# Eight experts placed by token count, three of them in positions of 64 seats with two products per weight tile

## What is computed

```
logits = h @ w_router                      # 256 x 8
top_v, top_i = top_k(logits, 2)
combine = sum(one_hot(top_i) * softmax(top_v))
out = sum over e of combine[:, e] * ((silu(h @ w1[e]) * (h @ w3[e])) @ w2[e])
```

## Time and profile before

| | us |
|---|---|
| Median of 3 runs (1662.18 to 1662.34) | 1662.2 |
| Span of the profiled execution | 1660.5 |
| PE busy | 1644.2 |
| DVE busy | 1286.4 |
| ACT busy | 1058.6 |
| One pass of the experts' loop | 119.0 |

### The profile page before, as it was taken

How to read it: one execution, slowest core, us unless ns; L and a number is a source line. 1 busy time by engine, 2 the same in 40 slices (tenths; PEclk the granted TensorE clock), 3 DMA queues, 4 the chain that set the end, 5 groups by cost and what they waited for, 6 DMA issues and landing times.

```text
span 1660.5 us, 22803 instructions
## 1 busy us (share of the span) xinstructions
PE 1644.2 (99%) x8464; PEld 1397.3 (84%) x8464; DVE 1286.4 (77%) x1163; ACT 1058.6 (64%) x961; POOL 30.1 (2%) x57
## 2 busy tenths in 40 slices
PE   9999999999999999999999999999999999999997
PEld 8988889999899888788888888888888888888885
DVE  7575567555567747698888888988888888888997
ACT  6654445434465544577777777777777777777775
POOL 1000000000000000010000000000000000000100
PEclk9999999999999999999999999999999999999999
DMA  7753488885365444799999999999999999999994
GB/s 233 231 188 121 150 279 298 264 263 189 103 207 191 140 139 165 253 379 393 395 394 386 357 394 388 359 391 385 364 384 376 375 392 364 387 388 360 394 392 160
DMA packets 243426, 496.98 MB, mean 299 GB/s; under 512 B 8534, under 2 KB 64400, under 8 KB 243360
## 3 DMA queue, kind: packets, MB, share of 16 engines
q1 hardware_dynamic: 237360, 479.23, 80.3%
q0 software_dynamic: 2624, 8.45, 1.5%
q10 hardware_dynamic: 3376, 8.39, 1.3%
HBM read 476.64 MB, written 19.40 MB: 299 GB/s over the span
## 4 chain that ended last, share of the span: by engine, by line
PE 91%; DVE 3%; ACT 3%; issue 2%; DMA 1%; SPq 1%; DVEq 0%; POOL 0%; ACTq 0%
PE bank L1142 25%; PE bank L681 20%; PE bank L1175 19%; PE bank L1146 12%; PE bank L852 9%; PE bank L1159 1%; ACT whi L1423 1%; PE bank L671 1%; DVE wlo L1804 1%; PE bank L966 1%; DMA x_sb<-in_x 1%; DMA hn<-in_mem 1%; ACT pbuf L1558 0%; SPq L1297 0%; PE bank L938 0%
## 5 line engine op out<-in xcount | busy, mean ns | idle before, releaser
L2219 DVE TENSOR_TENSOR wlo<-raw,whi 128x2048 fp32r<-128x2048 f32 x328 | 748.2, 2289 | 108.1 <-ACT whi L1660 108.1
L1660 ACT ACTIVATE whi<-raw 128x2048 fp32r<-128x2048 f32 x328 | 627.8, 1918 | 177.5 <-PE bank L1146 93.7
L1804 DVE TENSOR_TENSOR wlo<-raw,whi 128x2048 fp32r<-128x2048 f32 (+3 forms) x121 | 259.3, 2148 | 175.8 <-ACT whi L1423 174.0
L1142 PE MATMUL bank<-whi,yT_hi 128*128 128x512 f32 x896 | 352.5, 396 | 0.0
L1142 PE MATMUL bank<-whi,yT_lo 128*128 128x512 f32 x896 | 347.4, 390 | 0.0
L1423 ACT ACTIVATE whi<-raw 128x2048 fp32r<-128x2048 f32 (+3 forms) x121 | 217.8, 1801 | 137.4 <-PE bank L681 100.5
L1146 PE MATMUL bank<-wlo,yT_hi 128*128 128x512 f32 x896 | 240.0, 390 | 0.0
L1146 PEld LDWEIGHTS bank<-wlo,yT_hi 128*128 128x128 f32 x896 | 168.2, 188 | 35.5
L1142 PEld LDWEIGHTS bank<-whi,yT_lo 128*128 128x128 f32 x896 | 168.3, 188 | 33.7 <-DVE yT_lo L2187 0.2
L1142 PEld LDWEIGHTS bank<-whi,yT_hi 128*128 128x128 f32 x896 | 168.3, 188 | 33.5
L1175 PE MATMUL bank<-whi,yT_hi 128*128 128x512 f32 x448 | 176.1, 393 | 0.0
(11 more groups left out here) (287 smaller groups left out, 2014.0 us busy)
## 6 DMA issues: line engine op xcount, KB each, us to landing
raw<-in_moe_w SPq DMA_DIRECT2D x336, 1024.0 KB, 7.4
raw<-in_w_in SPq DMA_DIRECT2D x36, 1024.0 KB, 5.2
raw<-in_dense_w SPq DMA_DIRECT2D x30, 1024.0 KB, 6.5
raw<-in_w_br SPq DMA_DIRECT2D x12, 1024.0 KB, 5.0
raw<-in_w_out SPq DMA_DIRECT2D x8, 1024.0 KB, 5.1
rows_by_slot<-qxT SPq DMA_DIRECT2D x15, 512.0 KB, 7.0
raw<-in_w_mkv SPq DMA_DIRECT2D x6, 1024.0 KB, 8.4
y_by_slot<-qxT SPq DMA_DIRECT2D x9, 512.0 KB, 7.7
```

The costliest lines, as they stand in the source:

```text
L1142: nc.tensor.matmul(b[:, :], hselT[a][:, half, tok(k)], w[:, k, :], start=(half + k + a == 0), stop=False)
L1660: nc.scalar.activation(whi[:, (E0 + n) % SPLIT, :], raw[:, n % RAW, :], ACT.Copy).then_inc(hi_ready, 1)
L1804: V.tensor_tensor(wlo[:, m % SPLIT, 0:size], raw[:, pieces[n][1], 0:size], whi[:, m % SPLIT, 0:size].bitcast(F32), ALU.subtract).then_inc( ...
L2219: V.tensor_tensor(wlo[:, s, :], raw[:, n % RAW, :], whi[:, s, :].bitcast(F32), ALU.subtract).then_inc(lo_ready, 1)
```

## The change

Experts are no longer taken in the order of their numbers. DVE counts each expert's tokens, ranks the experts (expert 0 is put first whatever its count) and gives the five highest the five positions marked H of `"HLHLHLHH"` and the three lowest the three marked L. SP reads the expert's number for each position from memory and loads that expert's weights.

An H position works as before. An L position has 64 seats: its stationary tile holds the high parts of 64 tokens in columns 0 to 63 and their low parts in columns 64 to 127. One matmul with `whi` and one with `wlo` then stand in for three, and the results of seat s and of seat s + 64 have to be added. For the hidden values that is done on PE: ACT and DVE copy both up products out of PSUM as they are, eight matmuls of 64 columns with the constant matrix `fold` transpose and add them, then ACT applies Silu (`silu_t`), DVE multiplies (`gated_t`), ACT makes the high part and DVE the low part. For the result y it is done by two matmuls with `fold` in the next position's first block. The loop is gone: all positions are written out. The part for tokens beyond an expert's seats (128 or 64) has 16 passes, and is run if any expert has such tokens.

The core of the diff:

```diff
+LIGHT = 64
+ROLES = "HLHLHLHH"
...
+                    if is_light(phase):
+                        order = [(k, 0) for k in range(4)]
...
+            def hidden_T(phase, b_, j=0):
+
+                read(pe, (phase, "e3", b_), j)
+                if is_light(phase):
+                    read(pe, (phase, "e1", b_))
+                    pe.wait_ge(fold_ready, 1)
+                b = claim((phase, "eT", b_), j)
+                if is_light(phase):
+                    for i, src in enumerate((silu_m, g32_m)):
+                        for c in range(BM):
+                            a = (i * BM + c) * LIGHT
+                            ins = nc.tensor.matmul(b[:, a:a + LIGHT], src[:, tok(c)], fold[:, 0:LIGHT],
+                                                   start=True, stop=True)
...
+                    terms = ((0, 0), (0, 1)) if is_light(phase) else ((0, 0), (1, 0), (0, 1))
...
+            def fold_result(p):
+
+                for n in range(2):
+                    read(pe, (p, "ey", n))
+                    b = claim((p, "yf", n))
+                    mark(nc.tensor.matmul(b[:, :], fold, y_slot[:, n * HALF:(n + 1) * HALF], start=True, stop=True),
+                         (p, "yf", n))
...
+            up(0, "w1", 0, 0, lambda half: read(pe, ("rows0", l, half)))
+            up(0, "w3", 0)
+            for p in range(NE):
+                blocks(p)
+                if p < LAST:
+                    up(p + 1, "w1", 0, 0, lambda half: read(pe, (p + 1, "rows", half)))
+                    hidden_T(p, NM - 1)
+                    up(p + 1, "w3", 0)
+                    down(p, NM - 1)
...
+            expert = {0: 0}
+            for n in range(HEAD + EARLY, N_E):
+                p = e_items[n][0]
+                if p not in expert:
+                    sp.wait_ge(order_known, 1)
+                    expert[p] = sp.value_load(order_i[0:1, p:p + 1], min_val=0, max_val=NE - 1)
+                load_item(n, expert[p])
...
             reached(pool, ("mT", 0, 3))
+            nc.gpsimd.memset(fold, 0.0).then_inc(pool_step, 1)
+            for i, shift in enumerate((0, LIGHT, -LIGHT)):
+                pool.wait_ge(pool_step, 3 + ROPE // 2 + i + 1)
+                ins = nc.gpsimd.affine_select(out=fold, in_=fold, compare_op=ALU.not_equal, fill=1.0, base=shift,
+                                              pattern=[[-1, P]], channel_multiplier=1)
+                ins.then_inc(pool_step, 1) if i < 2 else ins.then_inc(fold_ready, 1)
             for t in range(T):
...
+                free(nc.scalar.activation(silu_m, b[:, :], ACT.Copy if is_light(phase) else ACT.Silu), (phase, "e1", b_))
+
+            def silu_folded(p, b_):
+
+                b = full(act, (p, "eT", b_))
+                nc.scalar.activation(silu_t, b[:, 0:BM * LIGHT], ACT.Silu).then_inc(silu_t_ready, 1)
+
+            def hidden_hi(phase, b_, j=0):
+
+                if is_light(phase):
+                    read(act, (phase, "eT", b_))
+                    nc.scalar.activation(by_slot(gated_m[0][:, b_ % 2, :])[:, :, 0:LIGHT],
+                                         gated_t.rearrange("p (c s) -> p c s", c=BM), ACT.Copy).then_inc(g_hi, 1)
+                    return
...
+                    e_hi(e_room(phase, "e1", b_), j)
+                    if is_light(phase):
+                        e_hi(e_room(phase, "eT", b_ - 1), j)
+                        silu_folded(phase, b_ - 1)
...
+            b = full(dve, ("most", l))
+            free(V.tensor_copy(load, b[:, 0:NE]), ("most", l))
+            read(dve, ("most", l))
+            square_e = [P, NE, NE]
+            link(V.scalar_tensor_tensor(out=key_e, in0=iota_e[:, :], scalar=-1.0 / 16, in1=load, op0=ALU.mult, op1=ALU.add))
+            link(V.tensor_scalar(key_e[:, 0:1], key_e[:, 0:1], 4096.0, None, ALU.add))
+            link(V.tensor_tensor(pairs_e, key_e.unsqueeze(1).broadcast_to(square_e),
+                                 key_e.unsqueeze(2).broadcast_to(square_e), ALU.is_gt))
+            link(V.tensor_reduce(order_e, pairs_e, AX_X, ALU.add))
+            link(V.tensor_tensor(pairs_e, iota_e[:, :].unsqueeze(1).broadcast_to(square_e),
+                                 order_e.unsqueeze(2).broadcast_to(square_e), ALU.is_equal))
+            dve.wait_ge(seats, NE)
+            link(V.tensor_tensor(pairs_e, pairs_e, seat[:, :].unsqueeze(1).broadcast_to(square_e), ALU.mult))
+            link(V.tensor_reduce(pos_e, pairs_e, AX_X, ALU.add))
+            link(V.tensor_scalar(cap_e, order_e, float(HEAVY), float(LIGHT - CAP), ALU.is_ge, ALU.mult))
+            link(V.tensor_scalar(cap_e, cap_e, float(CAP), None, ALU.add))
+            link(V.tensor_tensor(hits_e, iota_e[:, :].unsqueeze(2).broadcast_to(square_e),
+                                 pos_e.unsqueeze(1).broadcast_to(square_e), ALU.is_equal))
+            link(V.tensor_tensor(hits_e, hits_e, iota_e[:, :].unsqueeze(1).broadcast_to(square_e), ALU.mult))
+            link(V.tensor_reduce(order_f, hits_e, AX_X, ALU.add))
+            V.tensor_copy(order_i[:, :], order_f).then_inc(order_known, 1)
...
+                    free(V.tensor_copy(g32_m, b[:, :]), (phase, "e3", b_))
+                    return
...
+                    dve.wait_ge(silu_t_ready, light_block(phase, b_))
+                    free(V.tensor_tensor(gated_t, silu_t, b[:, BM * LIGHT:2 * BM * LIGHT], ALU.mult), (phase, "eT", b_))
+                    dve.wait_ge(g_hi, count)
+                    part = by_slot(gated_m[0][:, b_ % 2, :])
+                    V.tensor_tensor(part[:, :, LIGHT:2 * LIGHT], gated_t.rearrange("p (c s) -> p c s", c=BM),
+                                    part[:, :, 0:LIGHT].bitcast(F32), ALU.subtract).then_inc(g_lo, 1)
+                    return
```

559 lines of the change are left out of this document (309 added, 250 removed).

## The result

The changed kernel takes **1665.74 us** (median of 16 runs, 1663.17 to 1670.71) against 1662.19 before (16 runs, 1661.97 to 1662.68): ratio 1.0020, 95% interval 1.0014 to 1.0027. It is slower by 3.5 us, just over the 0.2% that I called measurable; I had forecast 1662.0. Not only the median moved: the runs of before lie within 0.7 us of each other, those of after within 7.5. The profiled execution took 1664.32 us, its span is 1662.5.

The account below looks back on a forecast made before the run. PE was taken to bound the kernel, with DMA close behind. L positions -5.4, router +3.2 and POOL +2.0 summed to -0.2 us: no change, 1662.0 us against 1662.2, range 1652 to 1673.

Parts of the forecast that it names:

- What bounds the kernel before: Expert stage: PE busy for all of a 119.0 us pass; DMA could not go below 114.2 us.
- L block 16.5 us in place of 16.86, not 11.8: L positions: a DVE and ACT hand-over loop sets 16.5 us a block, though PE would need only 11.8.
- I give back 0.3 us for each: Each way out of an L position: 0.3 us lost to a low-part wait and PE's foldings of y.
- Forecast -5.4: Three L positions: 6.3 us saved, less 0.3 us at each way out, -5.4 us.
- At nothing: the loops that go: Expert positions: writing out the loops changes nothing, since a branch costs nothing that shows.
- The router +3.2: Before the positions: 29 small DVE operations instead of 9 delay the fourth weight piece and PE, +3.2 us.
- POOL +2.0: POOL: making fold ahead of the second load of mem delays that load and PE, +2.0 us.
- Rival 2: L blocks: PE's idle time drops its clock to 1.2 GHz, +141 us, 1809 us in all; chance 0.03.
- Rival 1: L blocks: DVE and ACT wait 0.5 us more, 17.0 us a block, +10.5 us, 1672; chance 0.17.
- Rival 3: L positions: ACT splits a piece earlier, hiding the bubble; 14.4 us saved, 1653 or 1646 us; chance 0.13.

Follow-up runs that it names:

- experiment 1: The changed kernel with no L position (all eight positions H, still written out): 1666.94 us.
- experiment 2: The changed kernel with one ACT weight piece moved ahead of the high part of gated_t in every L block: 1644.63 us.
- experiment 6: The changed kernel without the overflow part and its branch on DVE: 1664.32 us; variants lengthened or cut the part.
- experiment 5: The changed kernel with DVE's routing operations moved behind the last weight pieces before the positions: 1668.05 us; cut into five parts instead: 1661.46 us.
- experiment 4: The changed kernel with fold's four POOL operations behind the second load of the memory rows: 1663.24 us.

## Why the prediction was wrong, point by point

The steps that failed are two that the sum put at nothing. The tail behind the branch had no term, and costs 1.65 us. And a wait of PE was priced at its own length: the fall of the clock behind it costs 1.6 us more after the router's wait in most executions, and one in the L positions 1.1 us. The rest of the sum comes out near the forecast, in part by luck.

- **What bounds the kernel before**: right, with one thing misread. "PE is busy for all of 119.00 us" doesn't exclude 0.5 us of slow starts in a pass (experiment 1).
- **L block 16.5 us in place of 16.86, not 11.8**: right, 16.51, by the loop named (experiment 2 removes it).
- **"I give back 0.3 us for each"**: wrong. Against the unrolled H pass of 118.5 the pair gives back 1.5 us on the H side; y's folding alone is two products that keep PE for 1.7 us, and I had priced the way out of an L position without a row for it. Forecast -5.4, measured -2.4. The H pass also holds the last L block: its folding of the hidden values, and a wait of 0.8 us. What part each has, no run shows.
- **"At nothing: the loops that go"**: wrong, -3.0 us. The two errors cancel, which is luck: the passes together gave -5.5.
- **The router +3.2**: its wait was 2.8 us (rightly placed, near 707), but the step ends there, and the clock's fall behind it costs 1.6 us more in most executions. No single term decides the sign: the profiled execution has the wait without this fall and is still 2.0 us slower than before, of which the tail is 1.65; and without the tail's wait the median is still 2.1 above before (experiment 6), while without the router's wait and its fall it is 0.8 below (experiment 5).
- **POOL +2.0**: right, 2.0 by experiment 4; +1.3 against before, for the 0.8 us gained earlier.
- **The tail**: not in the sum at all, +1.65 us. I had listed the overflow part nowhere, since it doesn't run. Another +0.7 are two stretches of slower starts on PE near 1551 and 1559, which before has not there; unexplained.
- **Rival 2, the clock**: dismissed at 0.03 because I priced it as all or nothing (+141 us). "Here bursts are longer than waits" is true and did not protect: one or two falls in an L position in 14 of 15 profiles, at 1.1 us for one of some 7 us. The Trainium skill ("TensorE: Matmul & The Clock Gate", HAM oscillation), which I had cited for it, describes bursts shorter than the waits; the runs have falls with waits of at most 2.0 us in an L block and longer bursts than that between them.
- **Rival 1**: did not come; the block takes 16.51 us, and ACT's high part starts 0.04 us behind the product's end (854.78 + 0.41 to 855.23).
- **Rival 3**: its price was low. Its condition (ACT splits a piece earlier) is experiment 2, and gave 1644.6, not 1653 or 1646 with +5.2 in the sum, since the pair of passes and not the single one is what the transfer bounds.

In sum: -0.8 (earlier start, no cause found) + 2.0 + 2.7 - 5.5 + 1.1 + 2.4 = +1.9 in the profiled executions, and 1.6 more in most others by the fall near 712, which makes the 3.5 of the medians. My -0.2 lacked the tail and the clock.

## What to carry to other kernels

When a change takes work off the engine that bounds, look at the loop of hand-overs that takes its place, and then at the order of the one queue in it: moving one piece ahead of a waiting operation was worth 21 us, six times what the whole change moved. Small operations on a feeding engine did best spread over the blocks where it has time; as one lump they held PE up in both places tried. And price the idle time that a change gives to PE as single falls of the clock behind single waits, beside the case in which it falls for good.

## What the runs showed of the hardware that I had not expected

- One wait of PE of 2.8 us in otherwise dense work brought the granted clock from 1.00 to 0.50 (2.4 to 1.2 GHz) in 9 of 11 profiles, and in none of the 7 without a wait there; it came back after some 3 to 4 us, and the fall cost 1.6 us beside the wait.
- In L blocks, with PE idle twice a block for at most 2.0 us, or, with ACT's order changed, mostly once for at most 2.5, one or two such falls came in 14 of 15 profiles, at places that vary; with matmuls in the gap ahead of the down product, in none of 2.
- The same 540 matmuls of a pass take 118.5 us as straight code and 119.0 as a loop pass.
- The transfer of weights keeps 394 GB/s over a pair of passes; a single pass can run ahead of it (109 us for 45.1 MB).
- A branch over code that doesn't run cost DVE 1.6 to 1.9 us or nothing, by what that code is and what stands ahead of it; 20 profiles, no rule.
